# Attention: the order of the units within a head, 4, 1, 3, 2 key pieces against 4, 1, 2, 3

## The reference

```python
def forgetting_attention(q, k, v, log_f):          # per block of 128 queries
    s = einsum('bqhd,bkhd->bhqk', q[:, q0:q1], k[:, :q1])
    bias = cum[q0:q1, None] - cum[None, :q1]
    p = softmax(where(causal, s + bias, -inf))
    out = einsum('bhqk,bkhd->bqhd', p, v[:, :q1])

def dilated_attention(q, k, v):                    # three windows, combined by their sums
    ...
```

## Time and profile before

| | |
|---|---|
| median of 3 runs | 1358.3 us (1351.87 to 1359.0) |
| the profiled execution | 1361.05 us |
| its span | 1359.4 us |
| TensorE busy | 1297.3 us, 95% of the span |
| VectorE, ScalarE, GpSimd busy | 561.1, 430.9, 335.6 us |
| attention stage | from 299.6 to about 512 us of the span |

### The profile page before, as it was taken

How to read it: one execution, slowest core, us unless ns; L and a number is a source line. 1 busy time by engine, 2 the same in 40 slices (tenths; PEclk the granted TensorE clock), 3 DMA queues, 4 the chain that set the end, 5 groups by cost and what they waited for, 6 DMA issues and landing times.

```text
span 1359.4 us, 18163 instructions
## 1 busy us (share of the span) xinstructions
PE 1297.3 (95%) x6732; PEld 1099.6 (81%) x6732; DVE 561.1 (41%) x1093; ACT 430.9 (32%) x844; POOL 335.6 (25%) x313
## 2 busy tenths in 40 slices
PE   6999999989999987999999999999999999999996
PEld 4899878878888876887788888888888888888885
DVE  7452544257777775674231121112111212121137
ACT  6323121246777773443212101210221022103122
POOL 6049522143555510000304100410221023002200
PEclk8899979999999998999999999999999999999998
DMA  5123333275555411233121102110311021012042
GB/s 194 63 68 89 126 79 140 93 189 183 139 141 144 102 31 62 78 93 109 47 93 47 47 1 93 46 46 0 108 46 31 0 108 46 31 38 86 17 160 103
DMA packets 41744, 112.72 MB, mean 83 GB/s; under 512 B 16678, under 2 KB 16726, under 8 KB 39756
## 3 DMA queue, kind: packets, MB, share of 16 engines
q1 hardware_dynamic: 36108, 94.30, 20.2%
q0 software_dynamic: 5296, 16.87, 6.5%
q10 hardware_dynamic: 288, 0.85, 0.2%
HBM read 87.27 MB, written 24.14 MB: 82 GB/s over the span
## 4 chain that ended last, share of the span: by engine, by line
PE 87%; DVE 5%; issue 3%; ACT 3%; DMA 1%; POOL 0%; DVEq 0%; ACTq 0%; SPq 0%; POOLq 0%
PE ps L1951 18%; PE ps L1934 12%; PE ps L1936 12%; PE ps L1935 12%; PE ps L1909 7%; PE ps L1820 3%; PE ps L401 3%; PE ps L403 3%; PE ps L402 3%; PE ps L1804 2%; PE ps L1703 2%; PE ps L1704 2%; PE ps L1705 2%; PE ps L1805 2%; PE ps L1840 1%
## 5 line engine op out<-in xcount | busy, mean ns | idle before, releaser
L1934 PE MATMUL ps<-op_hi,w_hi 128*128 128x512 f32 x704 | 274.2, 390 | 1.6 <-DVE ol L965 1.6
L1935 PE MATMUL ps<-ol,w_hi 128*128 128x512 f32 x704 | 274.1, 389 | 0.0
L1936 PE MATMUL ps<-op_hi,w_lo 128*128 128x512 f32 x704 | 274.1, 389 | 0.0
L1446 POOL TENSOR_TENSOR hid_lo<-hf,hid_hi 128x512 fp32r<-128x512 f32 x44 | 56.8, 1292 | 684.0 <-ACT hid_hi L916 684.0
L1934 PEld LDWEIGHTS ps<-op_hi,w_hi 128*128 128x128 f32 x704 | 132.2, 188 | 29.1 <-DVE ol L965 1.8
L1936 PEld LDWEIGHTS ps<-op_hi,w_lo 128*128 128x128 f32 x704 | 132.2, 188 | 27.5
L1935 PEld LDWEIGHTS ps<-ol,w_hi 128*128 128x128 f32 x704 | 132.2, 188 | 27.3
L383 DVE TENSOR_TENSOR w_lo<-w_raw,w_hi 128x1024 fp32r<-128x1024 f32 x44 | 57.8, 1315 | 212.9 <-ACT w_hi L378 212.9
L910 ACT ACTIVATE tg<-ps 128x512 f32<-128x512 f32 x44 | 26.4, 599 | 367.1 <-PE ps L1936 367.1
L965 DVE TENSOR_TENSOR z<-ps,z 128x512 f32<-128x512 f32 x80 | 51.5, 686 | 142.8 <-PE ps L1951 142.4
L1951 PE MATMUL ps<-wd_hi,hid_hi 128*128 128x512 f32 x352 | 108.5, 390 | 1.4 <-POOL hid_lo L1446 1.4
(11 more groups left out here) (269 smaller groups left out, 2447.2 us busy)
## 6 DMA issues: line engine op xcount, KB each, us to landing
w_raw<-w_stream SPq DMA_DIRECT2D x56, 512.0 KB, 3.3
wd_raw<-w_down SPq DMA_DIRECT2D x5, 2048.0 KB, 9.6
qk_scratch<-qk_hi SPq DMA_DIRECT2D x12, 512.0 KB, 2.6
qk_scratch<-qk_lo SPq DMA_DIRECT2D x12, 512.0 KB, 2.9
qa<-qk_scratch POOLq DMA_DIRECT2D x24, 256.0 KB, 4.2
ks<-qk_scratch POOLq DMA_DIRECT2D x24, 256.0 KB, 5.4
xt<-x_t SPq DMA_DIRECT2D x8, 512.0 KB, 8.1
wo_raw<-w_out SPq DMA_DIRECT2D x4, 1024.0 KB, 5.0
```

The source lines that it names most:

```text
L1446: return pool.tensor_tensor(out, a, b, op)
L1934: pe.matmul(out, w2_hi[:, j, k, :], op_hi[:, k, half(h)], start=k == 0, stop=False)
L1935: pe.matmul(out, w2_hi[:, j, k, :], ol[:, k, half(h)], start=False, stop=False)
L1936: last = pe.matmul(out, w2_lo[:, j, k, :], op_hi[:, k, half(h)], start=False, stop=k == KT - 1)
```

## The change

The last two units of each pass trade places: the unit with 2 key pieces is taken ahead of that with 3. All else follows from ORDER through PLACE, `unit`, `piece` and the lists BODY and PIECES. Units 3 and 0 keep their places, so both banks are still taken in turn. The number and the shapes of all instructions stay.

```diff
-ORDER = (3, 0, 2, 1)
+ORDER = (3, 0, 1, 2)
```

## The result

Over ten executions each, the changed kernel has a median of 1364.66 us (1360.82 to 1369.6), the one before 1358.53 (1350.88 to 1362.12). The ratio is 1.0069 with a 95% interval of 1.0044 to 1.0094: slower by about 0.7%. The profiled execution took 1369.37 us with a span of 1367.7, 8.3 more than the 1359.4 of before.

What follows compares the result with a forecast made beforehand. TensorE's fixed order of work was taken as the bound, only its waits moving. First pass -1.2, 11 periods +6.4 and drain +2.2 summed to +7.4 us, forecasting a median of 1365.7 us, range 1359 to 1373.

Steps and rivals of the forecast that it cites:

- Step 1: Three-piece unit (U3), second scores to first transposes: chain 2.56 us, cover falls to 0.99, loss 1.57, +1.14 us a pass.
- Step 2: Four-piece unit (U4): wait moves to U3's first output product, held by VectorE's y; 0.66 lost instead of 0.69, -0.03 us.
- Step 3: Two-piece unit (U2): chain needs 2.08 us, cover 2.00; 0.08 lost in place of 0.56, -0.48 us a pass.
- Sum for a masked pass: The three units' changed waits together make each masked pass +0.63 us longer.
- the term for the other kind of attention: Passes without the mask product: covers shorter, waits longer in both orders; 0.1 us taken off as an estimate.
- The ends: First pass and drain of the attention, priced apart from the periods between: -1.2 us and +2.2 us.
- the term of -1.2 for the first pass: First pass: narrower scores and a shorter chain ahead of its last unit save 1.2 us (0 to -1.6).
- the drain: From the last unit's first scores to the end of the last y: 9.84 us becomes 12.0, +2.2 (1 to 3).
- rival B: In every pass the new wait drops TensorE's clock to its lower level: +16 us, 1382 us; chance 0.07.
- Rival A: Not slower: freed waits outweigh U3's new one, a pass changes by -0.57 us, total -5.3 us, 1353; chance 0.10.
- Rival C: The order does nothing: the same 1.7 us of waits a pass, only elsewhere; 1358 to 1361 us, chance 0.08.
- the bound of no change: Whole kernel: a run can tell about 0.5% (6.8 us) from no change; chance of landing within it 0.44.

Runs made afterwards that it cites:

- the cast: Changed kernel with VectorE's cast of the next values moved from the four-piece unit's end to the one-piece unit's end: pass 17.66 us, ratio to before 1.0084.
- y first: Changed kernel with VectorE's final product (y) of the one-piece unit ahead of a piece's low half: pass 17.66 us, ratio to before 1.0047.
- the run again: The changed kernel run once more without any edit, against the kernel before: pass 17.66 us, median 1369.57 us, ratio 1.0102.

## Why the prediction was right, and where it wasn't

The forecast was +7.4 us; measured were +6.1 by medians, +9.4 by the ratio, +8.3 by the two profiled spans. The mechanism was right: work that lay under U3's chain was gone, and the experiments that gave work back took the loss away. Of the sum's terms one was mis-sized, that of the unmasked passes, and one of the ends can't be judged.

Step 1, U3's chain: said 2.56 us from the second S to T; measured 404.53 (0.07 behind the mask product at 404.46) to 407.10, 2.57, and 2.57 again in the other kind. The cover of 0.99 stands as said under a masked U4's S (an unmasked U4's S, without its mask products, is 0.93), and that it doesn't matter how the wait divides was shown by the cast. Right.

Step 2, U4's chain and y: said 2.47 and a loss of 0.66; measured 391.26 to 393.74, 2.48 and, less 1.85 of work, 0.63. That little depends on y was shown by y first, for which -0.1 us was expected and nothing came.

Step 3, U2's chain: said 0.08, measured 0.11 (400.85, where 400.74 was the pace). Right in the masked pass, the scaling to 512 columns too.

Sum for a masked pass: said +0.63, measured 1.58 + 0.63 + 0.11 less 1.68, +0.64. **What failed is the term for the other kind of attention**: the prediction took off 0.1 as an estimate, +0.53 in place of +0.63, and had no row for it. Two passes together take 35.32 us (387.39 to 422.71) where they took 33.96 (385.76 to 419.72), +1.36, so the unmasked one costs +0.72. The rows of that pass, first before, then after the change:

```profile
408.62 0.65 PE L1820 MATMUL ps<-ident,pr 128*128 128x128 f32 x4 [0.62 <-ACT pr L813]
...
416.02 0.65 PE L1820 MATMUL ps<-ident,pr 128*128 128x128 f32 x4 [0.39 <-ACT pr L813]
...
419.72 0.50 PE L1804 MATMUL ps<-ks,qa 128*128 128x512 f32 x1 [0.42 <-ACT pr L813]
```

```profile
418.53 0.65 PE L1820 MATMUL ps<-ident,pr 128*128 128x128 f32 x4
```

Against its pace TensorE loses 0.78, 0.56 and 0.58 us in it before, 1.92 where a masked pass lost 1.68. After the change it loses 1.64 at U3's chain (2.57 less 0.93 of cover), 0.71 at U3's first O (411.46) and 0.29 at T of U2's first piece (418.53, where 418.24 was the pace): 2.64 where a masked pass loses 2.32. Without the mask products there is less cover under chains of the same length, in both orders as the prediction said, but the changed order loses 0.32 more by it and the old one 0.24: the correction is about +0.1 and not -0.1. The rows of before lay in the same trace, one pass on. From the third pass to the twelfth, nine periods, 5.2 us were forecast and 5.9 came.

The ends: by the prediction's terms about 0 us up to U4's S of the third pass and +2.2 to +2.3 from that of the last pass on. Measured were +0.02, and +2.3 in the run where the clock stayed up, +3.5 in the changed kernel's profile. The first figure proves little. The run with the changed order in the last pass alone has the order of before in the first three, and took 34.02 us there against 35.35 in the profile of before, as TensorE was at the lower clock there for some 3 us in place of some 10 (estimates from the granted clock in stretches of 2 us). So the term of -1.2 for the first pass is neither confirmed nor refuted. The 1.2 us missing in the drain are rival B in a small place: not in the passes, where the clock stayed at 1.00 through 1.3 us of idle time in 6.0 (404 to 410 below), most of it between 404.5 and 407.1, but behind the last of them. There T of U3's first piece waits 2.41 us with no S of a next pass under it, and the next T are slow:

```profile
513.17 0.81 PE L1820 MATMUL ps<-ident,pr 128*128 128x128 f32 x4 [2.41 <-ACT pr L813]
...
514.64 1.05 PE L1820 MATMUL ps<-ident,pr 128*128 128x128 f32 x4
```

```profile
404.00:410.00 6.00, 4.68 (x31) 3.81 (x30) 4.18 (x10) 4.12 (x9) 5.92 (x9) 1.00 0.45 119
510.00:513.00 3.00, 0.77 (x5) 0.49 (x4) 1.51 (x5) 1.73 (x4) 0.00 (x0) 1.00 0.00 0
514.00:516.00 2.00, 2.00 (x11) 2.00 (x11) 0.69 (x1) 0.81 (x2) 0.00 (x0) 0.50 0.00 0
```

TensorE worked 0.77 of 3.00 us and then ran at the lower of its two levels, 1.2 in place of 2.4 GHz (0.50 from 514 to 516). In the run again, with the same 2.41 us of waiting (at 514.13), it didn't. The Trainium skill, "TensorE: Matmul & The Clock Gate", Part 1, has it that activity releases the throttle and idleness brings it back; the drain agrees, and its being met only now and then with the same wait agrees with the variation from run to run that the page describes. Part 4 says that transposes don't count as busy in the same way. Nothing of the kind shows in the passes, which have 36 transposes among some 120 products and stayed at 1.00.

Rival A is out: U3's chain in its new place measured 2.57, not 2.1, and with y ahead of the low half step 2 left as much as before. Rival C, that nothing happens, lay within reach of single medians but not of the passes.

What was right by luck: that it came out slower and not within the bound of no change. The sum of 7.4 lay only 0.6 beyond that bound of 6.8, and the two things that it had missed, in the unmasked pass and in the drain, both went upward.

## What to carry to other kernels

In a software pipeline written out by hand, list for each unit the length of the chain that its first consumer needs and the work that stands between; a new order is worth the change in the sum of the shortfalls. Here the unit whose scores were issued during the shortest unit, with the next unit short too, had the least cover, 0.99 us. When a wait is taken away, look at what else the moved instruction delays on every in-order queue it feeds: here 1.04 us more work under two waits was worth 0.30, and 0.64 once the cast was out of VectorE's queue. Take rows from each kind of pass that the loop holds, not from one.

## What the runs showed of the hardware

The printed idle time is no full account of lost pace. At a wait of T or S 0.16 us is missing (0.78 printed at 389.32, 0.94 lost), at a wait of O behind T 0.24 (0.39 printed at 393.74, 0.63 lost), and a pass without any printed idle time in it still ran 16.2 us, where the work of a pass at its pace is about 15.2 (15.46 masked, some 0.5 less without the eight mask products). And executions differ by 5 to 6 us through a stretch (150 to 200 us) in which all kernels here do the same work and TensorE is busy for 48.48 us, but the granted clock is 0.86 in five of the fourteen profiled executions and 1.00 in nine. In those five it fell to 0.50 within the 64 small products named above and stayed there for some 12 us of almost unbroken work, behind the same wait of 0.85 us. Why it falls in some executions and not in others stays open. A comparison of two orders by the distance between like instructions, behind that stretch, is free of it: the changed order's pass came out at 17.65 to 17.66 us in five profiled executions, two of the changed kernel and one each with y first, with the cast later and with the last pass in the old order.
